# Two FFN norms applied at the evacuation of the up products, sums spread into a GEMM, and the output stored in four pieces

## The reference, cut to what matters

```python
def rms_norm(x, g):
    y = x * lax.rsqrt(jnp.mean(x * x, axis=-1, keepdims=True) + EPS)
    return y * g
...
for l in range(DEPTH):                      # first block, DEPTH = 2
    h = rms_norm(h_res, attn_norm_g[l])
    z = h @ w_in[l]                         # c_q, c_kv, k_pe, rq, rk, rv, rg
    ...                                     # MLA and retention mixers -> y
    h_res = h_res + y @ w_out[l]
    hf = rms_norm(h_res, ffn_norm_g[l])
    gate, up = jnp.split(hf @ w_gate_up[l], 2, axis=-1)
    h_res = h_res + (silu(gate) * up) @ w_down[l]
return h_res[:, N_META:]
...
# second block: four modulated FFN steps, a pooling mixer, differential attention
return rms_norm_2(x, final_g)
```

## Time and profile before

| | us |
|---|---|
| median of 3 runs | 2307.53 |
| all runs | 2315.0, 2307.53, 2307.23 |
| profiled execution, its own time | 2313.31 |
| its span | 2311.6 |
| TensorE's mean granted clock, share of full | 0.992 |

### The profile page before, as it was taken

How to read it: one execution, slowest core, us unless ns; L and a number is a source line. 1 busy time by engine, 2 the same in 40 slices (tenths; PEclk the granted TensorE clock), 3 DMA queues, 4 the chain that set the end, 5 groups by cost and what they waited for, 6 DMA issues and landing times.

```text
span 2311.6 us, 37332 instructions
## 1 busy us (share of the span) xinstructions
PE 2270.2 (98%) x14214; PEld 2041.9 (88%) x14214; DVE 1440.6 (62%) x2240; ACT 831.1 (36%) x1117; POOL 163.1 (7%) x235
## 2 busy tenths in 40 slices
PE   8999999999999999999999999999999999999998
PEld 8999999998999988888888888898888888889998
DVE  4656776555777787578778767773333345556555
ACT  4444344444534432222432212233212234445433
POOL 0100000130000101001001001000000001000000
PEclk9999999998999999999999999999999999999999
DMA  5325665322565565455335545433232233123453
GB/s 220 110 73 174 214 234 183 124 83 101 197 239 195 178 207 181 165 194 175 105 130 206 181 166 196 157 108 109 82 106 103 74 108 110 56 73 131 172 190 126
DMA packets 65434, 343.20 MB, mean 148 GB/s; under 512 B 7104, under 2 KB 10432, under 8 KB 42560
## 3 DMA queue, kind: packets, MB, share of 16 engines
q1 hardware_dynamic: 44608, 266.47, 33.0%
q0 software_dynamic: 20736, 75.51, 9.7%
HBM read 340.90 MB, written 1.05 MB: 148 GB/s over the span
## 4 chain that ended last, share of the span: by engine, by line
PE 62%; issue 9%; DVE 3%; ACT 1%; POOL 0%; DMA 0%; POOLq 0%; DVEq 0%; ACTq 0%; SPq 0%
PE gpt L832 17%; PE gpt L834 17%; PE gpt L833 17%; DVE w_lo L1899 1%; PE gpt L759 1%; PE gpt L761 1%; PE gpt L760 1%; PE gpt L1314 1%; PE gpt L1315 1%; PE gpt L1316 1%; PE mbt L1356 1%; PE gpt L1297 1%; PE gpt L1299 1%; PE gpt L1298 1%; PE mbt L1376 1%
## 5 line engine op out<-in xcount | busy, mean ns | idle before, releaser
L832 PE MATMUL gpt<-xn_hi,w_hi 128*128 128x512 f32 (+2 forms) x2288 | 756.2, 331 | 2.2 <-DVE w_lo L1899 2.2
L833 PE MATMUL gpt<-xn_lo,w_hi 128*128 128x512 f32 (+2 forms) x2288 | 753.9, 330 | 0.0
L834 PE MATMUL gpt<-xn_hi,w_lo 128*128 128x512 f32 (+2 forms) x2288 | 753.9, 330 | 0.0
L1899 DVE TENSOR_TENSOR w_lo<-raw,w_hi 128x2048 fp32r<-128x2048 f32 (+2 forms) x280 | 567.7, 2028 | 260.8 <-ACT w_hi L1441 259.6
L1441 ACT ACTIVATE w_hi<-raw 128x2048 fp32r<-128x2048 f32 (+2 forms) x280 | 476.1, 1700 | 369.1 <-PE gpt L834 326.1
L832 PEld LDWEIGHTS gpt<-xn_hi,w_hi 128*128 128x128 f32 x2288 | 434.3, 190 | 41.2 <-DVE w_lo L1899 2.2
L834 PEld LDWEIGHTS gpt<-xn_hi,w_lo 128*128 128x128 f32 x2288 | 434.2, 190 | 37.6
L833 PEld LDWEIGHTS gpt<-xn_lo,w_hi 128*128 128x128 f32 x2288 | 434.3, 190 | 37.4
L832 PE MATMUL gpt<-mid_hi,w_hi 128*128 128x512 f32 (+2 forms) x996 | 333.0, 334 | 1.3 <-DVE mid_lo L2083 1.1
L833 PE MATMUL gpt<-mid_lo,w_hi 128*128 128x512 f32 (+2 forms) x996 | 332.3, 334 | 0.0
L834 PE MATMUL gpt<-mid_hi,w_lo 128*128 128x512 f32 (+2 forms) x996 | 332.3, 334 | 0.0
(11 more groups left out here) (325 smaller groups left out, 2627.8 us busy)
## 6 DMA issues: line engine op xcount, KB each, us to landing
raw<-in_up_a SPq DMA_DIRECT2D x72, 1024.0 KB, 4.8
ada_w<-in_ada POOLq DMA_DIRECT2D x144, 512.0 KB, 3.5
raw<-in_up_b SPq DMA_DIRECT2D x60, 1024.0 KB, 4.8
raw<-in_down_a SPq DMA_DIRECT2D x48, 768.0 KB, 4.3
raw<-in_down_b SPq DMA_DIRECT2D x48, 640.0 KB, 3.8
raw<-in_win SPq DMA_DIRECT2D x16, 1024.0 KB, 4.8
raw<-in_qkv SPq DMA_DIRECT2D x12, 1024.0 KB, 4.8
raw<-in_wout SPq DMA_DIRECT2D x8, 1024.0 KB, 4.8
```

The costliest lines, as they stand in the source:

```text
L832: mm(o, w_hi[b][:, j, :], hi(k), start=(k == 0), stop=False)
L833: mm(o, w_hi[b][:, j, :], lo(k), start=False, stop=False)
L834: last = mm(o, w_lo[b][:, j, :], hi(k), start=False, stop=(k == kt - 1))
L1899: V.tensor_tensor(w_lo[b][:, 0:tiles, :], raw[b][:, 0:tiles, :], w_hi[b][:, 0:tiles, :].bitcast(F32), ALU.subtract).then_inc(lo_ready, 1)
```

## The change

It has six parts. (a) For norms 1 and 3 (`LATE`), xn_hi and xn_lo are made from R times gain, without the norm's factor, right behind each out slot's residual (ACT with the gain as scale, DVE's `late_low`); `norm1` falls away there, and so do the `keep_clock` matmuls. xn is widened to 544 columns, so that these tiles and the mixers' outputs stand in different columns. (b) PE starts the first up slot at once, makes the norm's column sums behind it, and the row in the middle of the second (`between`). DVE copies the row to `ssum`, and each of the 44 up slots is evacuated by two DVE multiplications with it (`hidden_scaled`), a split of the next weights, and a third product (`hidden_product`). ACT's silu reads the scaled gate from SBUF and stands behind the split. (c) The latents' twelve sums go into the next GEMM, two behind each of its first k. (d) `k_part(0, 0)` waits per channel tile, with no `keep_clock(5)` ahead; DVE's split for it goes ahead of norm tiles 3 to 7, and ACT's share of these goes behind the split of the third q slot. (e) ACT applies the final gain ahead of the row; DVE multiplies by the row in four instructions of 512 columns; each is stored by a DMA of its own, of 256 KB. (f) Two small tiles are shared or cut.

```diff
-            sp.wait_ge(out_ready, KT)
-            sp.dma_start(out, R[:, :, N_META:T1]).then_inc(out_done, 16)
-            sp.wait_ge(out_done, 16)
+            for k in range(0, KT, 2):
+                sp.wait_ge(out_ready, k // 2 + 1)
+                sp.dma_start(out[:, k:k + 2, :], R[:, k:k + 2, N_META:T1]).then_inc(out_done, 16)
+            sp.wait_ge(out_done, 4 * 16)
...
+                        elif after in LATE:
+                            def late_rows():
+                                norm_rows(after)
+                                if after == 2 * DEPTH - 1:
+                                    context_rows()
+
+                            gemm_first(p0, 0, KT, 2, hi, lo, n, xn_ready, xi * KT)
+                            norm_sums(after)
+                            if after == 2 * DEPTH - 1:
+                                context_columns()
+                            gemm(p0, 1, KT, 2, hi, lo, n, between=late_rows)
...
+                lat_sums = [(j, t, k) for j in range(2) for t in range(len(TT1)) for k in range(LORA_T)]
+
+                def lat_thin(k):
+
+                    for j, t, i in lat_sums[2 * k:2 * k + 2]:
+                        t0 = TT1[t][0]
+                        last = mm(mb[0][:, 3 * j + t:3 * j + t + 1], qsq[:, 2 * j + i, t0:t0 + P], ones[:, 0:1],
+                                  start=(i == 0), stop=(i == 1))
+                        if (j, t, i) == lat_sums[-1]:
+                            last.then_inc(lat_col, 1)
+
                 pe.wait_ge(evac_done, done_at(base + 1))
-                for j in range(2):
-                    for t, (t0, _, _) in enumerate(TT1):
-                        for k in range(LORA_T):
-                            last = mm(mb[0][:, 3 * j + t:3 * j + t + 1], qsq[:, 2 * j + k, t0:t0 + P], ones[:, 0:1],
-                                      start=(k == 0), stop=(k == 1))
-                last.then_inc(lat_col, 1)
-                gemm(pl + 1, 1, KT, 2, hi, lo, T1)
+                gemm(pl + 1, 1, KT, 2, hi, lo, T1, thin=lat_thin)
...
-                first, second, third = FILL[2 * L + 1]
-                keep_clock(first, mb[1])
-                norm_sums(2 * L + 1)
-                if L == DEPTH - 1:
-                    context_columns()
-                keep_clock(second, mb[1])
-                norm_rows(2 * L + 1)
-                if L == DEPTH - 1:
-                    keep_clock(3, mb[0])
-                    context_rows()
-                keep_clock(third, mb[0])
...
                 for k in ks:
+                    if p == 0 and m == 0:
+                        pe.wait_ge(xc_ready, ctx_tiles(8) + k + 1)
...
-            keep_clock(5, mb[0])
-            pe.wait_ge(xc_ready, ctx_tiles(9))
             k_part(0, 0, range(KT))
...
+                    act.wait_ge(evac_done, done_at(s0 + g))
+                    for m in range(2 * g, 2 * g + 2):
+                        A(xn_hi[:, m, x], R[:, m, c0:c0 + n], ACT.Identity, scale=lv[:, V_FFN + m:V_FFN + m + 1])\
+                            .then_inc(xh_ready, 1)
+                    if g == 3:
+                        split(p + 1, b, tiles[g])
                     for m in range(2):
                         square(ni, 2 * g + m, s0 + g, m)
-                    if g == 3:
-                        split(p + 1, b, tiles[g])
...
                     with act.Fori(0, up - 1) as i:
                         for b in range(2):
-                            silu(p0 + i, b)
+                            if late is None:
+                                silu(p0 + i, i * 2 + b, b)
                             split(p0 + i + 1, b, SIDE_T)
+                            if late is not None:
+                                silu(p0 + i, i * 2 + b, b)
                             round_hidden(p0 + i, i * 2 + b, b)
...
+            for k in range(KT):
+                act.wait_ge(sq_ready, summed(10) + k + 1)
+                r = R[:, k, N_META:T1]
+                A(r, r, ACT.Identity, scale=vec2[:, W_FIN + k:W_FIN + k + 1]).then_inc(fin_gain, 1)
...
+                    def hidden_scaled(p, j, b):
+
+                        dve.wait_ge(slot_done, done_at(2 * p + b))
+                        V.tensor_tensor(sg[:, b, 0:n], gp[b][0][:, 0:n], ssum[:, 0:n], ALU.mult).then_inc(gate_scaled, 1)
+                        V.tensor_tensor(midf[:, b, 0:n], gp[b][1][:, 0:n], ssum[:, 0:n], ALU.mult).then_inc(evac_done, 1)
+
+                    def hidden_product(p, j, b):
+                        dve.wait_ge(sg_ready, j0 + j + 1)
+                        dve.wait_ge(evac_done, done_at(2 * p + b))
+                        V.tensor_tensor(midf[:, b, 0:n], midf[:, b, 0:n], sg[:, b, 0:n], ALU.mult).then_inc(mid_f, 1)
...
-                        if 2 * g + m < KT - 1:
+                        if g < 3:
                             add_square(ni, 2 * g + m, m)
-                norm_columns(ni)
-                if tiles[2] is None:
-                    dve.wait_ge(lo_ready, done_at(s0 + 4))
+                        late_low(ni, 2 * g + m)
                 split(p + 1, b, tiles[3])
+                add_square(ni, KT - 2, 0)
+
+            def late_low(ni, m):
+
+                c0, n = NORMS[ni]
+                x = slice(LATE_X[ni], LATE_X[ni] + n)
+                dve.wait_ge(xh_ready, ni * KT + m + 1)
+                V.scalar_tensor_tensor(xn_lo[:, m, x], R[:, m, c0:c0 + n], col(lv, V_FFN + m), xn_hi[:, m, x].bitcast(F32),
+                                       ALU.mult, ALU.subtract).then_inc(xn_ready, 1)
+
+            def late_row(ni):
+
+                n = NORMS[ni][1]
+                dve.wait_ge(row_ready, whole(ni) + 1)
+                V.tensor_copy(ssum[:, 0:n], mb[1][:, 0:n]).then_inc(rrow_ready, 1)
+                dve.wait_ge(rrow_ready, LATE.index(ni) + 1)
...
-            norm2_half(8, 1, range(3, KT))
+            scaled_half(8, 1, 3)
+            scaled_half(8, 1, 4)
+            split(k_slot(0) // 2, 0, SIDE_T)
+            lo_half(8, 1, 3)
+            for k in range(5, KT):
+                scaled_half(8, 1, k)
+                lo_half(8, 1, k - 1)
+            lo_half(8, 1, KT - 1)
...
-            for k in range(KT):
-                V.scalar_tensor_tensor(R[:, k, N_META:T1], R[:, k, N_META:T1], col(vec2, W_FIN + k), mb[1][:, 0:SEQ],
-                                       ALU.mult, ALU.mult).then_inc(out_ready, 1)
+            for k in range(0, KT, 2):
+                dve.wait_ge(fin_gain, k + 2)
+                r = R[:, k:k + 2, N_META:T1]
+                V.tensor_tensor(r, r, mb[1][:, 0:SEQ].unsqueeze(1).to_broadcast([P, 2, SEQ]), ALU.mult).then_inc(out_ready, 1)
```

More of the change, by code:

```diff
@@ L322, in build, with tiled @@
         FILL = {0: (5, 3, 3), 1: (3, 3, 3), 2: (2, 2, 6), 3: (3, 1, 0), 9: (2, 3, 4), 10: (0, 2, 0)}
+        LATE = (1, 3)
+        LATE_X = {1: T1, 3: 0}
+        Y_AT = (0, SEQ - N_META)
+        def tiled(ni):
+            return (ni - sum(ni > j for j in LATE)) * KT
         CTX_NORM = 4
@@ L826, in gemm @@
                         pe.wait_ge(lo_ready, done_at(s))
+                    if m == 1 and between is not None:
+                        between()
                     o = gp[b][m][:, 0:n]
@@ L834, in gemm @@
                         last = mm(o, w_lo[b][:, j, :], hi(k), start=False, stop=(k == kt - 1))
+                        if thin is not None and m == 0:
+                            thin(k)
                 last.then_inc(slot_done, 1)
@@ L843, in ffn @@
             def ffn(p0, f, xi, n, after, before=None):
-                hi, lo = xn(0, n)
+                hi, lo = xn(LATE_X.get(after, 0), n)
                 mh, ml = mid(n)
@@ L2087, in ffn @@
                         for b in range(2):
-                            hidden(p0 + i, i * 2 + b, b)
+                            if scaled_by is None:
+                                hidden(p0 + i, i * 2 + b, b)
+                            else:
+                                hidden_scaled(p0 + i, i * 2 + b, b)
                             split(p0 + i + 1, b, SIDE_T)
+                            if scaled_by is not None:
+                                hidden_product(p0 + i, i * 2 + b, b)
                             hidden_lo(i * 2 + b, b)
@@ L2092, in ffn @@
                     for b in range(2):
-                        hidden(p0 + up - 1, 2 * up - 2 + b, b)
+                        if scaled_by is None:
+                            hidden(p0 + up - 1, 2 * up - 2 + b, b)
+                        else:
+                            hidden_scaled(p0 + up - 1, 2 * up - 2 + b, b)
                         split(p0 + up, b, cnt)
+                        if scaled_by is not None:
+                            hidden_product(p0 + up - 1, 2 * up - 2 + b, b)
                         hidden_lo(2 * up - 2 + b, b)
@@ L2438, in layer1 @@
                 ffn(pl + S_FFN1 // 2, L, OUT_TOK[L][1], plain_residual(L), [SIDE_T, SIDE_T], 2 * L + 2,
-                    late=() if L < DEPTH - 1 else (lambda_products,))
```

(2 more changed lines are left out.)

82 lines of the change are left out of this document (51 added, 31 removed).

## The result

The changed kernel takes 2332.45 us (median of 4 runs, 2327.17 to 2333.99) against 2307.66 before: a ratio of 1.0083 with a 95% interval of 1.0059 to 1.0107, some 14 to 25 us slower (19 by the ratio itself; the two medians are 24.8 apart). The forecast was 2301. The profiled execution took 2333.99, with a span of 2332.3 (before: 2313.31 and 2311.6).

The account below looks back on a forecast made before the run. The prediction took TensorE, busy for 98% of the span, as the bound. FFNs +4.6 and -7.0, latent sums +3.0, k_part +3.2 and the end +2.6 made +6.4, so 2307.5 becomes 2301.1 us; range 2294.0 to 2309.0.

Parts of the forecast that it names:

- the sum: Whole kernel: 4.6 - 7.0 + 3.0 + 3.2 + 2.6 = 6.4 us gained.
- The ring (b): Up loops: a chain of waits through ACT and DVE per pair of slots; PE waits if it exceeds PE's pair.
- The ring is 13.0: Layer 1's up_a loop, with a table load ahead of the split: 13.0 us against PE's 11.52, 1.5 lost per pair.
- Together 11.7: Up loops without that table load: the ring's halves, 5.0 and 6.7 us, make 11.7 a pair.
- the cover is 0.3 a pair: Layer 0's up loop: the ring stays below PE's 12.03 us, so the loop costs nothing.
- rival (3): Up loops: DVE's chain is longer, handovers perhaps 0.1 us more each; 9.6 us lost, 2310.7; chance 0.14.
- The loads: Layer 1's up_a: two table loads a round; the one ahead of the split adds 1.3 us, silu's hides beneath w_lo.
- rival (4): Layer 1's up_a: each function change costs an unseen 1.4 us beyond its load; 11 us lost, 2312; chance 0.03.
- The clock (c): Latent sums: spreading them avoids PE's half clock, 1.5 us in each layer, 3.0 gained; bounds 0 and 3.
- rival (5): PE's clock drops at the new sums between up slots, or still at the latents'; 3 us lost, 2304; chance 0.16.
- (d): k_part: key matmuls follow the q slots directly, without fills; gain 3.2 us, bounds 1.5 and 3.2.
- (e): Kernel's end: four DVE instructions take 2.8 us, the last 256 KB store lands in 2.5; gain 2.6, bounds 1.9 and 3.5.

Follow-up runs that it names:

- wide: The kernel before with only xn_hi and xn_lo widened from 512 to 544 columns, two small tiles cut to make room: ratio 1.0072.
- shift: The kernel before with xn rows still 512 columns apart, but 1024 unused bytes behind xn_hi and behind xn_lo: ratio 0.9998.
- row528: The kernel before with xn rows 528 columns apart: ratio 1.0074 to the kernel before.
- flat: The changed kernel with the second block using xn's memory in rows of 512 columns (results not the reference's): ratio 1.0013 to the kernel before.
- after_again: The changed kernel executed a second time, nothing altered: 2328.43 us.
- before_again: The kernel before executed a second time, nothing altered: 2308.78 us.
- flat_silu: As flat, plus a one-column silu ahead of layer 1's FFN that takes the table loads out of its loop: ratio 0.9990 to the kernel before.
- mod_first: As packed_silu, with DVE's modulation moved ahead of mid_lo in the first block's up loops: ratio 0.9950 to the kernel before.
- no_late: Parts (c), (d), (e), (f) alone, both FFN norms as in the kernel before, xn rows 512 columns: ratio 0.9973 to the kernel before.
- packed_silu: The changed kernel with xn rows 512 columns from layer 1 on and a silu ahead of layer 1's FFN: ratio 1.0009 to the kernel before.

## Why the prediction was wrong

**The failed step is one that the sum lacks: the widened xn.** The text costs the instructions of parts (a) to (e) and says nothing of the allocation that (a) brings with it. It changes no instruction of the second block, and there it cost 17 us: 512-column matmuls of 0.2323 us in place of 0.2267. wide, shift, row528 and flat show it from both sides. None of the rivals had it, and the range reached only to what the loops might cost. With this term the sum would have been 6.4 - 17 = -10.6, about 2318.

**The ring (b): right mechanism, undersized.** "The ring is 13.0" was 13.45, "Together 11.7" was 12.15 in layer 1 and 12.23 in layer 0, where "the loop there costs nothing; the cover is 0.3 a pair" was false by 0.2 a pair. A round has four handovers between product, rounding and mid_lo, three of them in the ring, and I took an instruction's length for each; they measured 0.55 and 0.57, some 0.13 more, 0.4 a pair. That is rival (3) at about its size (0.1 per handover), which got 0.14. Layer 0's FFN won 2.7 to 3.4 where the sum had 4.6, layer 1's lost 16.4 (15.8 in after_again) where it had 7.0. Layer 1's by parts, from DVE's splits of the same tiles in the two traces (the first part starts at 562.38 before and at 556.81 after):

| part of layer 1's FFN | before | after | lost | forecast |
|---|---|---|---|---|
| head | 19.77 | 17.70 | -2.1 | -4.2 |
| loop of up_a | 51.84 | 60.80 | +9.0 | +6.9 |
| end of up_a | 15.42 | 15.89 | +0.5 | +1.5 |
| down_a | 31.42 | 34.65 | +3.2 | 0 |
| up_b | 46.00 | 48.84 | +2.8 | +0.6 |
| end of up_b, down_b | 44.55 | 47.55 | +3.0 | +2.2 |

Of the 9.4 over the forecast the two loops are 4.3, about nine rounds of 0.4, and that is the ring. The 3.2 of down_a are not: before_again, without the change, has 33.75 there, and flat_silu, with it, 31.43. Of the head's 2.1, 1.5 are half clock (below). So is part of the last line, which the text didn't have at all: the wait for mid_lo at the end of up_b is 3.1, and TensorE's clock behind it is half, at a cost of some 1.6.

```profile
749.40 0.39 PE L844 MATMUL gpt<-mid_hi,w_hi 128*128 128x256 f32 x1 [3.10 <-DVE mid_lo L2140]
...
749.00:753.00 4.00, 3.60 (x18) 3.60 (x19) 3.42 (x7) 2.51 (x4) 0.00 (x0) 0.59 0.49 164
```

All six traces with norm 3 late have such a stretch there (waits of 2.7 to 3.2), the eight others (0.8 to 0.9) none. These 9.4 and the 1.9 that layer 0 missed bring 2318 to 2329, against a median of 2332.45 and executions from 2327.17 to 2333.99. mod_first confirms the ring: cutting 0.75 out of it (12.16 to 11.41) took the loops' waits away.

**The loads.** The load ahead of the split lies in the ring and the one ahead of silu does not, as said; together they cost 5.3 (flat to flat_silu, 5.2 in the traces; the sum had 1.3 for each of four pairs, 5.2). No drain showed: the load starts 0.02 behind the rounding's end and the split 1.29 behind the load's start, so rival (4)'s extra 1.4 is excluded here. By the Trainium skill (ScalarE: Activation LUTs, What ACT_TABLE_LOAD costs) it would have been 2.66 for a switch of set. The trace disagrees: neither load of a round takes more than its own 1.29, nor do the two loads around the Exp of the earlier trace rows in the kernel before, where the function changes twice (784.71 to 786.00 and 786.32 to 787.61).

**The clock (c) and rival (5).** The gain was counted as 3.0, the upper one of its bounds. Where the drop came it cost 1.5: between DVE's two splits around layer 0's sums there are 10.23 in the kernel before, 8.69 in before_again and 8.71 in the changed kernel. It came at 6 places in 10, so the spread sums are worth 1.8 on average. Rival (5) came true at one of the two late norms, slot 1 of layer 1 behind the sums; the changed kernel:

```profile
568.20:571.80 3.60, 3.60 (x21) 3.60 (x21) 0.16 (x1) 2.01 (x2) 1.89 (x3) 0.58 0.90 339
```

A granted clock of 0.58 over 3.6 us costs some 1.5. Five of the six traces with norm 3 late have it there, but so do two of the eight without, behind the same sums in their old order (before_again and no_late). Layer 0's head, at full clock, took what was worked out: slot 2 starts 15.5 after 186.50 and takes 6.0, 21.5 in all.

```profile
202.03 0.39 PE L844 MATMUL gpt<-xn_hi,w_hi 128*128 128x272 f32 x1 [0.75 <-DVE w_lo L1945]
```

**(d) and (e): right.** The key GEMM follows its forerunner at once:

```profile
1956.38 0.27 PE L846 MATMUL gpt<-xn_hi,w_lo 128*128 128x256 f32 x1
1956.49 0.40 PE L1318 MATMUL gpt<-xn_hi,w_hi 128*128 128x512 f32 x1
```

That gave 3.3 (3.2 forecast). At the end DVE took 2.48 (2.8), a piece landed in 2.8 (2.5), and from DVE's start to the end of the span went 5.7 us where it was 8.3: 2.5 won (2.6 forecast). By the fixed cost of a DMA in the Trainium skill (DMA: Bandwidth & Descriptors, Anatomy of one DMA; fitted there on GpSimd's path) the prediction estimated about 2 us of gain from the split store; the traces agree, with 2.8 for a piece of 256 KB against 4.6 for 1024 KB, 1.8 less.

The balance of the profiled executions: +17.0 rows, +16.4 layer 1's FFN, -2.7 layer 0's, -3.3 k_part, -2.5 the end, -1.4 of the 256-column matmuls in the last FFN (faster with the wide rows), -2.8 in the mixers and latents, mostly clock stretches: +20.7, the difference of the spans.

## What to carry to other kernels

A new shape of a tile has a cost even where no instruction that uses the tile changes: count the matmuls in an equal window before and after, since a slower stream shows as neither wait nor idle time. When work moves into a loop in which two engines hand tiles to and fro, add up the ring with the starts of measured handovers, not with lengths, and look for work that can fill the handover: a modulation moved by one line was worth 8 us by the traces (packed_silu to mod_first). And before counting a saved half-clock stretch, look at more than one execution of the kernel.

## What the runs showed of the hardware

- A matmul that streams 512 fp32 columns takes 0.2267 us with tile rows 2048 bytes apart (10.88 for 48), 0.2317 with 2112 bytes (11.12) and 0.2323 with 2176 (11.15), at the same granted clock; start addresses of whole tiles moved by 1024 and 2048 bytes don't matter. With 256 columns the wide rows are faster, 0.118 against 0.120 (5.65 and 5.76 for 48). Which property of the rows does it, their distance or where each of them starts, wasn't separated.
- A table load costs its 1.28 us and nothing more: in layer 1's loop the load starts 0.02 behind the end of the instruction ahead of it, and the one behind it starts 1.29 to 1.30 after the load's start.
- A handover from DVE to ACT or back, for an instruction of 0.42, takes 0.55 to 0.57 from start to start.
- The same program, executed twice, had half-clock stretches of different length at the same places of its mixers (0.63 and 0.82 mean granted clock over 18.5 us); several us of difference between two single traces can come from this alone.
- A wait of TensorE of 2.7 to 3.2 us between the up_b and down_b slots of layer 1 went with a half-clock stretch at its end in all six traces that have it (0.59 mean granted clock over 4 us in the changed kernel); the eight traces with a wait of 0.8 to 0.9 there have none.
